# Values of four heads token-major, heads in pairs, and an out-projection with a 512-column operand

## The reference, cut to what matters

```python
q, k, v, g = jnp.split(h @ a_w_in[layer], 4, axis=-1)             # layer 0
o = chunked_relbias_attention(...)                                # scores + bias, softmax, @ v
x = x + (o * jax.nn.silu(g)) @ a_w_out[layer]
# layer 1: k, v = h_kv @ kv_w; q, g = h @ b_w_in; forgetting_attention; x + (o * silu(g)) @ b_w_out
```

## Time and profile before

| | |
|---|---|
| three runs | 2741.17, 2743.82, 2750.49 us; median 2743.82 |
| the profiled execution | 2735.26 us, its span 2733.6 us |
| PE busy | 2601.8 us, 95% of the span |
| PE weight load busy | 2335.0 us, 85% |
| DVE, ACT, POOL busy | 1836.8 (67%), 1381.5 (51%), 340.4 (12%) us |
| mean granted clock | 0.984 |
| memory | 161 GB/s over the span |

### The profile page before, as it was taken

How to read it: one execution, slowest core, us unless ns; L and a number is a source line. 1 busy time by engine, 2 the same in 40 slices (tenths; PEclk the granted TensorE clock), 3 DMA queues, 4 the chain that set the end, 5 groups by cost and what they waited for, 6 DMA issues and landing times.

```text
span 2733.6 us, 47989 instructions
## 1 busy us (share of the span) xinstructions
PE 2601.8 (95%) x16826; PEld 2335.0 (85%) x16826; DVE 1836.8 (67%) x2701; ACT 1381.5 (51%) x2186; POOL 340.4 (12%) x371
## 2 busy tenths in 40 slices
PE   6999997688999999999999999999999999999997
PEld 6999994586888898898889889788988898898887
DVE  7888886447866656656665666666666656666664
ACT  5445457344545545545554445555455545544454
POOL 3111015431300000000000000111010101000102
PEclk9999999898999999999999999999999999999999
DMA  7656650007666666666676666567666767676763
GB/s 196 181 161 176 174 154 18 14 4 191 182 170 174 167 174 184 175 178 172 168 190 174 174 171 173 153 167 192 177 182 166 176 187 178 176 179 170 187 179 93
DMA packets 855527, 441.46 MB, mean 161 GB/s; under 512 B 28176, under 2 KB 851472, under 8 KB 855472
## 3 DMA queue, kind: packets, MB, share of 16 engines
q1 hardware_dynamic: 850320, 430.16, 58.6%
q0 software_dynamic: 5152, 10.56, 2.4%
HBM read 437.35 MB, written 3.31 MB: 161 GB/s over the span
## 4 chain that ended last, share of the span: by engine, by line
PE 71%; DVE 3%; ACT 1%; issue 1%; DMA 0%; POOL 0%; DVEq 0%; SPq 0%; POOLq 0%; ACTq 0%
PE bank L255 35%; PE bank L256 18%; PE bank L237 4%; PE bank L238 4%; PE bank L236 4%; PE bank L1453 1%; DVE vT L1675 1%; DVE vT L1673 1%; PE bank L1468 1%; PE bank L1448 1%; ACT cross L1541 1%; PE bank L1459 1%; PE bank L1469 1%; PE bank L1447 1%; PE bank L1434 0%
## 5 line engine op out<-in xcount | busy, mean ns | idle before, releaser
L255 PE MATMUL bank<-xx,hib 128*128 128x512 f32 x4352 | 1568.6, 403 | 15.7 <-DVE lob L220 11.5
L256 PE MATMUL bank<-xx,lob 128*128 128x256 f32 x4352 | 1217.6, 280 | 0.0
L220 DVE TENSOR_TENSOR lob<-rawb,hib 128x1024 fp32r<-128x1024 f32 x672 | 829.6, 1242 | 412.0 <-ACT hib L213 402.9
L255 PEld LDWEIGHTS bank<-xx,hib 128*128 128x128 f32 x4352 | 820.0, 188 | 203.9 <-DVE lob L220 17.0
L213 ACT ACTIVATE hib<-rawb 128x1024 fp32r<-128x1024 f32 x672 | 700.8, 1055 | 501.4 <-PE bank L256 325.8
L256 PEld LDWEIGHTS bank<-xx,lob 128*128 128x128 f32 x4352 | 823.4, 189 | 2.2 <-issue 0.5
L236 PE MATMUL bank<-xh,hia 128*128 128x258 f32 (+2 forms) x1040 | 299.3, 288 | 12.2 <-DVE xl L372 12.2
L237 PE MATMUL bank<-xl,hia 128*128 128x258 f32 (+2 forms) x1040 | 295.7, 284 | 0.0
L238 PE MATMUL bank<-xh,loa 128*128 128x258 f32 (+2 forms) x1040 | 294.8, 283 | 0.0
L236 PE MATMUL bank<-oh,hib 128*128 128x256 f32 x1024 | 290.4, 284 | 0.0
L238 PE MATMUL bank<-oh,lob 128*128 128x256 f32 x1024 | 289.8, 283 | 0.0
(11 more groups left out here) (302 smaller groups left out, 2393.5 us busy)
## 6 DMA issues: line engine op xcount, KB each, us to landing
rawb<-in_a_w_in_dram SPq DMA_DIRECT2D x256, 512.0 KB, 5.2
rawa<-in_w_in_dram SPq DMA_DIRECT2D x130, 512.0 KB, 5.0
rawb<-in_b_w_in_dram SPq DMA_DIRECT2D x128, 512.0 KB, 5.2
rawb<-in_kv_w_dram SPq DMA_DIRECT2D x128, 512.0 KB, 5.2
rawb<-in_a_w_out_dram SPq DMA_DIRECT2D x64, 512.0 KB, 5.0
rawb<-in_b_w_out_dram SPq DMA_DIRECT2D x64, 512.0 KB, 4.9
rawb<-in_w_out_dram SPq DMA_DIRECT2D x32, 512.0 KB, 5.4
table<-in_rel_dram POOLq DMA_DIRECT2D x32, 128.0 KB, 5.5
```

The costliest lines, as they stand in the source:

```text
L220: nc.vector.tensor_tensor(self.lo[b][:], self.raw[at.u % RAW][:, h * HALF:(h + 1) * HALF], self.hi[b][:].bitcast(F32), ALU.subtract).then_ ...
L255: nc.tensor.matmul(out[:], self.hi[b][:, w], both, start=h == 0 and k == 0, stop=False)
L256: last = nc.tensor.matmul(out[:, 0:SEQ], self.lo[b][:, w], xx[:, 8 * h + k, 0], start=False, stop=h == 1 and k == 7)
```

## The change

It has three parts.

1. **Values.** The 8 heads of a group become 2 blocks of `VB = 4`. A block begins with four units of value weights, each holding 4 of the 16 tile rows with all 512 columns of the four heads. `unit_turned` makes x the stationary operand and the weights the moving one: for each tile row and each half of the tokens three products of 512 columns, accumulated over all four units in two banks of their own (`VO`, psum 6 and 7). ACT copies each with the inverse norm as a per-token scale (`invc`) into `vtm`. The norm is turned from a row to a column by POOL through memory, once per layer. The transposes of the values, vT and its evacuation go.
2. **Pairs.** The other 12 units of a block are two times q_a, k_a, q_b, k_b, g_a, g_b. The attention of a head lies a unit behind, as PE's program below shows. ACT and DVE have the order given.
3. **Out-projection.** `oh` and `ol` become one tensor `oo`; a tile is one product of 512 columns and one of 256 (`wide`). Each unit's two outputs take a bank each, psum 0 to 3, and DVE adds main and cross sums to x1 in two instructions of 512. The first unit of a group waits for the evacuation of the last g_b. The sum for the forget gates moves from P2 to the bank OT.

The counting of banks goes by units that use them (`At.e`, `free`, `emptied`), since value units use none.

In the diff, cut to its core, the two programs of a pair on ACT and DVE are written several calls to a line, without their shared arguments.

```diff
+        def wide(self, pe, at, h, out, both, start, stop, tiles=range(8), before={}):
+            b = (2 * at.u + h) % SPL
+            if start and tiles[0] == 0:
+                wait(pe, taken[at.bank()], at.free())
+            pe.wait_ge(lo_ready, at.count(2 * at.u + h + 1, 2))
+            for k in tiles:
+                if k in before:
+                    before[k]()
+                w = slice(k * P, (k + 1) * P)
+                nc.tensor.matmul(out, self.hi[b][:, w], both(k).rearrange("p a t -> p (a t)"), start=start and k == 0,
+                                 stop=False)
+                last = nc.tensor.matmul(out[:, 0:SEQ], self.lo[b][:, w], both(k)[:, 0], start=False,
+                                        stop=stop and k == 7)
+            if k == 7:
+                last.then_inc(half_used, 1)
...
+        def unit_turned(self, pe, at, quarter, xx, outs):
+            for h in range(2):
+                b = (2 * at.u + h) % SPL
+                pe.wait_ge(lo_ready, at.count(2 * at.u + h + 1, 2))
+                for k in range(2):
+                    kt = 4 * quarter + 2 * h + k
+                    w = slice(k * 4 * P, (k + 1) * 4 * P)
+                    for t, out in enumerate(outs):
+                        tokens = slice(t * P, (t + 1) * P)
+                        nc.tensor.matmul(out, xx[:, kt, 0, tokens], self.hi[b][:, w], start=kt == 0, stop=False)
+                        nc.tensor.matmul(out, xx[:, kt, 1, tokens], self.hi[b][:, w], start=False, stop=False)
+                        last = nc.tensor.matmul(out, xx[:, kt, 0, tokens], self.lo[b][:, w], start=False,
+                                                stop=kt == KT - 1)
+                last.then_inc(half_used, 1)
...
+                    def weigh(j):
+                        def emit():
+                            pe.wait_ge(v_taken, block_no(layer, g, b) * 2 + 2)
+                            pe.wait_ge(pt_taken, head_no(layer, g, b, j) + 1)
+                            pe.wait_ge(og_ready, head_no(layer, g, b, j) + 1)
...
+                    for v in range(VB):                                          # PE, a block
+                        st.unit_turned(pe, place(layer, g, b, v), v, xx[src[2]], VO)
+                    for p in range(VB // 2):
...
+                        st.unit_wide(pe, q_a, xq)
+                        st.unit_wide(pe, k_a, xk)
+                        st.unit_wide(pe, q_b, xq, ({}, {0: scores(j_a, q_a, k_a)}))
+                        st.unit_wide(pe, k_b, xk, ({}, {0: turn_probs(j_a)}))
+                        st.unit_wide(pe, g_a, xg, ({4: weigh(j_a)}, {0: scores(j_b, q_b, k_b)}))
+                        st.unit_wide(pe, g_b, xg, ({}, {0: turn_probs(j_b), 5: weigh(j_b)}))
...
                     for m in range(GH):                                          # PE, project
-                        at = place(layer, g, n=4 * GH + m)
+                        at = place(layer, g, n=m)
                         if m == 0:
-                            pe.wait_ge(ol_ready, head_no(layer, g, GH - 1))
+                            other = at + -1
+                            pe.wait_ge(taken[other.bank()], other.evacuated())
+                            pe.wait_ge(ol_ready, head_no(layer, g, 0, GH - 1))
...
+                    def gate(at, j):                                             # ACT
+                        move_cross(at)
+                        act.wait_ge(taken[at.bank()], at.evacuated())
+                        a(eg[:], gT[:], ACT.Tanh, scale=0.5).then_inc(gate_ready, 1)
+                        act.wait_ge(og_ready, head_no(layer, g, b, j) + 2)
+                        dst = oo[:, bass.ds(b * VB + j, 1), 0, :].rearrange("p a t -> p (a t)")
+                        a(dst, og[:], ACT.Copy).then_inc(oh_ready, 1)
...
+                    for t in range(2):
+                        a(vtm[:, t], VO[t], ACT.Copy, scale=invc[:, t:t + 1]).then_inc(v_taken, 1)
...
+                        split(q_a); move_cross(q_a); split(k_a); move_cross(k_a)   # ACT, a pair
+                        split(q_b); exps(j_a); move_cross(q_b)
+                        split(k_b); take_probs(j_a); move_cross(k_b)
+                        split(g_a); exps(j_b); gate(g_a, j_a)
+                        split(g_b); take_probs(j_b); gate(g_b, j_b)
...
+                        split(q_a); evacuate(q_a); split(k_a); evacuate(k_a)       # DVE, a pair
+                        split(q_b); maxima(j_a); shares(j_a); evacuate(q_b)
+                        split(k_b); evacuate(k_b)
+                        split(g_a); maxima(j_b); shares(j_b); evacuate(g_a); gate(j_a)
+                        split(g_b); evacuate(g_b); gate(j_b)
...
-                            tt(xs, GB[at.bank()][:], xs, ALU.add).then_inc(taken[at.bank()], 1)
+                        pair = x1[:, 2 * m:2 * m + 2]
+                        sums = banks[:, 2 * at.bank():2 * at.bank() + 2]
+                        tt(pair, sums[:, :, 0:SEQ], pair, ALU.add).then_inc(x1_half, 1)
+                        dve.wait_ge(x1_half, g * GH + (m + 1 + AH * layer))
+                        tt(pair, sums[:, :, SEQ:], pair, ALU.add).then_inc(taken[at.bank()], 1)
```

More of the change, by code:

```diff
@@ L1392, in head, with heads @@
                                          ALU.add).then_inc(masked, 1)
+                def heads(g, b):
+                    for j in range(VB):
+                        head(g, b, j)
                 def project(g):
@@ L1438, in _ @@
                     src = [1, 0, 0, 1]
[L1440 to L1469, removed]
@@ L1471, in project @@
                 def project(g):
                     def product(at, half, tiles):
[L1473 to L1476, removed]
+                        st.wide(pe, at, half, psum[2 * at.bank() + half], lambda k: oo[:, k], start=True, stop=True,
+                                tiles=tiles)
@@ L1489, in project @@
                                 product(at, half, range(8))
-                layers(pe, layer, head, project)
+                layers(pe, layer, heads, project)
             total(2)
@@ L1534, in _, with heads, split @@
                     a(fz[:, 2], fz[:, 2], ACT.Ln).then_inc(f_ln, 1)
-                def head(g, h):
-                    n = head_no(layer, g, h)
-                    q, k, v, gg = (place(layer, g, h, m) for m in range(4))
+                def heads(g, b):
+                    def split(at):
+                        ahead(split_hi, at, 0)
+                        ahead(split_hi, at, 1)
                     def move_cross(at):
@@ L1592, in project @@
                         finished(g, GH - 1)
-                layers(act, layer, head, project)
+                layers(act, layer, heads, project)
             root(2)
@@ new lines, in heads @@
+                    for v in range(VB):
+                        split(place(layer, g, b, v))
+                    for p in range(VB // 2):
+                        q_a, k_a, q_b, k_b, g_a, g_b = (place(layer, g, b, n + 6 * p) for n in range(VB, VB + 6))
+                        j_a, j_b = 2 * p, 2 * p + 1
+                        split(q_a)
+                        evacuate(p, U_QA, q_a, qT)
+                        split(k_a)
+                        evacuate(p, U_KA, k_a, kT)
+                        split(q_b)
+                        maxima(j_a)
+                        shares(j_a)
+                        evacuate(p, U_QB, q_b, qT)
+                        split(k_b)
+                        evacuate(p, U_KB, k_b, kT)
+                        split(g_a)
+                        maxima(j_b)
+                        shares(j_b)
+                        evacuate(p, U_GA, g_a, gT)
+                        gate(j_a)
+                        split(g_b)
+                        evacuate(p, U_GB, g_b, gT)
+                        gate(j_b)
```

336 lines of the change are left out of this document (195 added, 141 removed).

## The result

The changed kernel takes 2809.19 us (median of 4 runs, 2803.36 to 2815.80) against 2743.14 for the kernel before beside it: a ratio of 1.0236, 95% interval 1.0205 to 1.0268. It is 66 us slower, where I had forecast 32 and a range that ended at 2812: the right side, half the size. The profiled execution had 2815.8 us.

A forecast was written before the change was run, and what follows sets the result against it. PE was taken as the bound, busy 1931 of 1957 us in the attention layers. Terms -52.5 -9.4 +80 +12.4 +3 +0.7 -1 gave +33 us, so 2768 or 2777; forecast 2775, range 2755 to 2800 (60%), outer 2738 to 2812.

The forecast's parts named there:

- turning of the values gone: Per head, four transposes of the values and the wait before them go, 0.78 us, 64 times, plus 2.6: -52.5 us.
- value products: Per block of four heads, 96 products of 512 columns at 0.2333 us replace 64 pairs: no change, ends -10 and +11.
- the pairs that stay in the heads: Pairs of 512- and 256-column products left in the heads, taken at 0.350 us a pair as before: 0.
- wait for the probabilities of b: PE stands 2.48 us for ACT's copy before weighing each b head, 32 times: +80 us, ends +64 to +96.
- out-projection, seven groups: Pairs of products replace triples, 46.15 to 44.8 us a group, -1.35 each: -9.4 us in seven groups.
- wait for g_b: First out-projection unit of each group waits 1.55 us for g_b's evacuation, 8 groups: +12.4 us.
- ends of layers 0 and 1, start of layer 0: Lateness at layer 0's end +3 us, longer add at layer 1's end +0.7, shorter wait at layer 0's start -1.
- granted clock: No term in the sum; 8 x 1.7 = 14 us more at the group ends allowed within the range.
- chain of ten steps: Walk along ACT's and DVE's queues from scores b: PE can weigh b at 10.81 us, wanted at 8.33.
- Rival 1: Weighing b isn't late in ACT's queue; everything but this wait sums to -47 us, giving 2697; 14%.
- rival 3: Each new PE stall brings a stretch at clock 0.50, 1.7 us more, 32 times: 54 us, 2830; 7%.
- the ring: Layer 0's last group: add, square, gained copies, low parts, split depend in a circle; saving lost, up to 5.8 us late: +3.

The follow-up runs named there:

- experiment 1: Changed kernel plus ten unread 512-column products on PE in front of the weighing of every b head; 2775.18 us, 1.0123 of before.
- experiment 2: Also the second kernel: changed kernel with ACT's copy of b's turned probabilities moved between tanh and og copy of head a's gate; 2713.48 us, 0.9893 of before.
- experiment 3: Changed kernel with the same ACT copy moved only past g_b's two splits, to behind head a's whole gate; 2721.05 us, 0.9926 of before.
- experiment 5: Changed kernel with only the wait for g_b's evacuation at a group's first out-projection unit taken out; 2787.24 us, 1.0196 of before.
- the fourth kernel: Kernel of experiment 2, also without the wait for g_b's evacuation at a group's first out-projection unit; 2684.31 us, 0.9787 of before.
- after again: The changed kernel run and profiled once more, unaltered; 2800.9 us in one run, layers 2045.8 us.
- experiment 7: The fourth kernel with the out-projection's 512-column product as two of 256 columns for 7 of 8 tiles; 2718.05 us, 0.9939 of before.

## Why the prediction was right and where it was wrong

By its own steps; the measured ledger of the layers (profiles, after less before) adds up to 65 of 67.1 us; 2 more lie in experiment 1, whose own two stops at the jumps of layer 1 make its gain look that much smaller.

| step | predicted | measured |
|---|---|---|
| turning of the values gone | -52.5 | -52.3 |
| value products | 0 (-10 to +11) | -10 |
| the pairs that stay in the heads | 0 | +6 |
| wait for the probabilities of b | +80 | +77 |
| out-projection, seven groups | -9.4 | -6 |
| wait for g_b | +12.4 | +14.6 |
| ends of layers 0 and 1, start of layer 0 | +2.7 | about +5 |
| granted clock (experiment 1: layers of 2049.8 and 2019.0 us) | 0, in the range up to +14 | +31 |

- **The wait, right.** The chain of ten steps held to 0.07 us at each of them, and experiments 2 and 3 move it as the walk says. Rival 1 was false in the changed kernel; what it said of the sum without this wait was too low: the second kernel, which lacks it, took 2713 and not 2697, for the longer waits for g_b and their half clock.
- **The clock, wrong: the term that failed.** I held rival 3 at 7%, "against: 2.5 us is shorter than both", and let half clock in only at the group ends. The one wait of 2.9 us in before had kept the clock, and I read a bound from a single case. The waits of 2.5 us are followed by 3.4 us or more at half clock in 17 of 32 cases (20 in the second profile of the same kernel, 15 in experiment 5); not in each, as rival 3 had it. I summed a stall at its length when it also has a price in clock, sometimes. Experiment 1 prices that at 31 to 34 us, the missing half. Which of the waits of 2.5 us set it off stays open.
- The Trainium skill (TensorE: Matmul & The Clock Gate, "Why this matters for your kernels") allows gaps up to some 3 us. Here the trace disagrees: gaps of 2.45 to 2.7 us were enough in about half the cases. Gaps of up to 1.94 (experiment 1, group ends) and 0.75 us (experiment 3) were not in any.
- **The value products, at the cheap end.** They start 0.227 us apart and a block takes 21.8 us, exactly 0.2133 plus the 0.0135 that the out-projection's row gave; I took 0.2333 from the 512-column product inside a pair, whose start is pushed by its neighbour.

```profile
863.09 0.40 PE L295 MATMUL bank<-hib,xx 128*128 128x512 f32 x1
863.32 0.40 PE L296 MATMUL bank<-hib,xx 128*128 128x512 f32 x1
863.56 0.39 PE L297 MATMUL bank<-lob,xx 128*128 128x512 f32 x1
863.78 0.39 PE L295 MATMUL bank<-hib,xx 128*128 128x512 f32 x1
```

The Trainium skill (TensorE: Matmul & The Clock Gate, "Back-to-back issue gap") has 2.5 ns beside the columns for a product in isolation. Here it is 13.5 ns; the measurement decides.
- **The pairs, a miss that hid this.** A pair takes 0.347 or 0.353 us. Before, heads of the two kinds were mixed, 24.67 and 25.00 us, 0.350 a pair in the mean; in the profile of after the mean is 0.352, and in the fourth kernel every pair is of the slower kind (a block's twelve units take 74.36 us, 16 times of 16), 9 us in all. Why is open; nothing I ran separates it.
- **The wait for g_b** was 1.8 us in the mean instead of 1.55 (the terms as I gave them add up to 1.50). At full clock, in experiment 1, it is 1.55 at the last group of each layer, whose code stands outside the group loop, and 1.82 at the six others: there PE starts 0.33 us after the evacuation's end instead of 0.06. Why is open. Half clock adds 0.14 in three cases. The wait could be left out altogether, which I had not asked. The out-projection gained less than summed because its pairs too ran at 0.353 in the profile of after; in the second profile of the same kernel four groups ran at 0.347, so this term moves by itself.
- **The ends**: the ring shows as waits of 0.8 to 0.9 us at three units of layer 0's last group, and the last norm comes 0.72 us later, as forecast.

## What to carry to other kernels

When a piece of work is moved behind another on an in-order engine, walk both queues with measured durations to the place where the bottleneck waits, and look at what stands in front of the small copy that it needs: here two weight splits of 1 us each, needed much later, stood in front of a copy of 0.5 us needed at once. A move of one call turned 66 us lost into 28 won, and leaving out a wait that nothing needed made it 56. A stall of the matrix engine costs more than its length where it is long enough to pull the clock down; a filler of useless products in its place, at unchanged waits, measures how much. One undisturbed gap of 3 us is no proof that gaps of 2.5 us are safe.

## What the runs showed of the hardware that I had not expected

- The clock's answer to a gap isn't a matter of its length alone. Gaps on PE from start to start, and how many were followed by a stretch at 0.50: 0.6 to 0.75 us, 0 of 32 (experiment 3); 1.67 to 1.94 us, 0 of 8 (experiment 1); 2.45 to 2.7 us, 17, 20 and 15 of 32 (after, after again, experiment 5), and 2 of 8 at the group ends of experiment 3; 2.6 to 3.2 us, 5 of 8 (experiment 2); one of 3.18 us in before, none; 3.5 us and more, at the start of layer 0 in all 12 profiles and at the jumps of experiment 7, 16 of 16. Two gaps of 1.2 and 1.3 us close together, once of nine.
- Products of 512 columns of this type with a new stationary operand each time start 0.227 us apart, those of 256 columns 0.120: a fixed 0.0135 us beside the columns at 2.4 GHz.
- With 112 products more in a loop's body on PE, four stops of about 4 us came at its jumps back, with 20 more two of 1.0 and 1.3 us, with neither none. The cause is not shown.
- The same pairs of products, at a clock of 1.00 and without waits, took 0.347 or 0.353 us in different stretches of one kernel. What decides is open.
